# x queued first, rotary tables made later, 12 taps of a matrix tile on VectorE, statistics products inside z chunks

## The chip, the core and the metric

The kernel runs on one core of a Trainium2 chip. The metric is the device time of one execution, in microseconds (us). TensorE (PE in the profile) multiplies matrices; VectorE (DVE), ScalarE (ACT) and GpSimd (POOL) work on tiles of 128 partitions; SyncE (SP) issues all the loads and stores.

## The reference, cut

A convolution layer, then an attention layer. Only the first is touched, and the rotary tables of the second.

```python
def conformer_conv_branch(h, w_in, b_in, conv_w, conv_b, norm_g, norm_b, w_out, b_out):
    proj = h @ w_in + b_in                     # (512,1024) @ (1024, 3*2048)
    val, glu_gate, z = jnp.split(proj, 3, axis=-1)
    u = val * jax.nn.sigmoid(glu_gate)
    u = lax.conv_general_dilated(u, conv_w[:, None, :], ...) + conv_b   # depthwise, causal, 31 taps
    u = jax.nn.silu(layer_norm(u, norm_g, norm_b))                      # over the 2048 channels
    u = u * jax.nn.silu(z)
    return u @ w_out + b_out
def rope_tables(positions, dtype):
    freqs = ROPE_THETA ** (-jnp.arange(0, 64, 2, dtype=jnp.float32) / 64)
    ang = positions.astype(jnp.float32)[..., None] * freqs
    return jnp.cos(ang).astype(dtype), jnp.sin(ang).astype(dtype)
```

## The kernel before, in words

Channels lie on partitions and the 512 positions on the free axis, so the 2048 channels of the convolution are 16 tiles. Each fp32 product is made of three matmuls: the operands are split into a high part (ScalarE copies to fp32r, `w_hi`, `xt_hi`) and the rest (GpSimd subtracts, `w_lo`; VectorE, `xt_lo`). The weights come in chunks of 128 columns, 512 KB each: SyncE loads a chunk into one of two raw buffers once both splits of the chunk before last are done, ScalarE makes `w_hi` (line 710), GpSimd `w_lo` (line 566), and TensorE spends 24 matmuls of 512 columns on it (`columns`, matmuls at line 1416). The slots of `w_hi` and `w_lo` are four. All orders are written by hand, one program for each engine, with semaphores between them.

**Start.** SyncE queues x in four parts with the first two weight chunks between them, then the taps (`taps_raw`, 31 rows of 8 KB), six small vectors (`vec_raw`), `freq` and the positions (`pos_int`, broadcast to 128 partitions). All nine small transfers count on one semaphore, `small_landed`. TensorE turns x with 32 transposes, does chunk 0, then `small_transposes` (16 of the taps at line 1434, one of the vectors at 1437), which waits for all nine, then chunk 1. ScalarE evacuates the turned taps and vectors (`conv_w_hi`, `vec`), which the biases of the first evacuation need. VectorE makes the angles of the rotary tables in 13 chained operations (lines 1045 to 1059), then copies the taps (1062, 1063), then begins to convolve. ScalarE makes `sin` and `cos` from the angles.

**Value and gate.** For tile t, chunk 2t gives `val` and chunk 2t+1 `sig` (ScalarE), and GpSimd multiplies them to `u` (line 571).

**Convolution.** 12 of the 16 tiles are convolved on VectorE, one instruction a tap (line 1093), two tiles at a time taking turns, but the first 14 taps and the last dozen run as one chain. Tiles 3 and 9 are shared: ScalarE multiplies (744), GpSimd adds (593). Tiles 12 and 13 are convolved on TensorE after chunk 31: each tap is a diagonal matrix, three matmuls, 31 taps, in four groups (`convolve`); GpSimd makes `diag_hi` (606) and ScalarE `diag_lo` (753). VectorE adds up all tiles (`csum`, lines 1076 and 1078).

**z chunks and statistics.** TensorE does 16 chunks of z. Ahead of chunk 10 it sums `csum` over the channels (line 1488), ahead of chunk 13 the squares (1495), ahead of chunk 14 it spreads the reciprocal deviation (1481). In between VectorE centres the tiles (1146), ScalarE squares them (814), VectorE adds the even squares (1152) and GpSimd the odd ones (621), GpSimd takes the power (642) and ScalarE makes `rstd_diag` (853).

**Branch and output projection.** For each tile VectorE scales (1176), ScalarE does silu (820), VectorE multiplies with z (1183), ScalarE makes `g_hi` (826), VectorE `g_lo` (1187). The output projection takes two tiles of g for each chunk of weights; in the loop of 16 tiles ScalarE also splits output chunks 2 and 3, and the chunks from 4 on come after it.

## Time and profile before

| | |
|---|---|
| median of 3 runs | 876.32 us (876.02 to 878.18) |
| the profiled execution: time | 877.75 us |
| the profiled execution: span from first to last instruction | 876.0 us |
| mean granted TensorE clock | 0.995 |
| TensorE busy | 851.5 us, 97% of the span |
| VectorE, ScalarE, GpSimd busy | 601.8, 398.2, 471.8 us |

The span is what the profile's clock covers; 1.75 us of the execution lie around it. TensorE's busy share is near the whole, so what matters is which of its gaps go and which come, and how many matmuls it has to do.

### The profile page before, as it was taken

The numbers are of one execution on the slowest core, as the hardware profiler recorded it, in microseconds if no ns is written. First come the engines' busy times: TensorE is split into PE (matmuls) and PEld (weight loads), VectorE is DVE, ScalarE is ACT, GpSimd is POOL, SyncE is SP. The second block draws the span as 40 slices with busy tenths as digits, with TensorE's granted clock in tenths as the row PEclk, the third lists the DMA queues.
The fourth block names the chain that finished last, engine by engine and source line by source line (L and its number), as shares of the span: only waits on it lengthen the run. The fifth ranks groups of instructions, "written<-read, shape, count | busy, mean of one in ns | idle before, by whom it ended". The sixth has DMA issues, their size and how long they took to land.

```text
span 876.0 us, 11846 instructions
## 1 busy us (share of the span) xinstructions
PE 851.5 (97%) x4083; PEld 708.4 (81%) x4083; DVE 601.8 (69%) x1089; ACT 398.2 (45%) x690; POOL 471.8 (54%) x260
## 2 busy tenths in 40 slices
PE   6999999999999999999999999999999999989996
PEld 5788888888888788788898788788888898878885
DVE  2899999999999749321723380157977878787207
ACT  3555444444564467431332443255555546554110
POOL 3577988896996572493454456142432433136431
PEclk9899999999999999999999999999999999999999
DMA  6232333330024323453143324323123230224212
GB/s 214 75 96 74 97 96 96 96 97 25 1 73 125 109 80 103 142 186 98 49 121 109 97 72 133 84 73 84 42 56 84 72 84 15 70 97 145 97 48 97
DMA packets 111399, 78.99 MB, mean 90 GB/s; under 512 B 14071, under 2 KB 98141, under 8 KB 111325
## 3 DMA queue, kind: packets, MB, share of 16 engines
q1 hardware_dynamic: 111356, 78.44, 30.2%
q8 instruction: 24, 0.39, 0.2%
q14 instruction: 19, 0.16, 0.1%
HBM read 71.87 MB, written 2.10 MB: 84 GB/s over the span
## 4 chain that ended last, share of the span: by engine, by line
PE 95%; DMA 2%; DVE 1%; SPq 1%; issue 1%; ACT 1%; DVEq 0%; ACTq 0%
PE bank L1416 89%; PE bank L1679 2%; DMA pos_int<-in_positions_dram 2%; PE bank L1668 1%; PE bank L1669 1%; PE bank L1554 0%; SPq L419 0%; DVE fg_lo L1400 0%; SPq L412 0%; PE bank L1434 0%; PE bank L1606 0%; PE bank L1495 0%; DVE pt_lo L1355 0%; SPq L416 0%; ACT prob L970 0%
## 5 line engine op out<-in xcount | busy, mean ns | idle before, releaser
L566 POOL TENSOR_TENSOR w_lo<-w_raw,w_hi 128x1024 fp32r<-128x1024 f32 x103 | 253.6, 2472 | 189.3 <-ACT w_hi L710 163.4
L1093 DVE SCALAR_TENSOR_TENSOR bank<-u,conv_w,bank 128x512 f32<-128x512 f32 x348 | 233.8, 759 | 0.9
L710 ACT ACTIVATE w_hi<-w_raw 128x1024 fp32r<-128x1024 f32 x103 | 107.0, 1054 | 117.6 <-PE bank L1416 66.8
L1416 PE MATMUL bank<-xt_hi,w_lo 128*128 128x512 f32 x384 | 153.6, 400 | 1.4 <-DVE xt_lo L1032 1.4
L1416 PE MATMUL bank<-xt_lo,w_hi 128*128 128x512 f32 x384 | 152.4, 397 | 0.0
L1416 PE MATMUL bank<-xt_hi,w_hi 128*128 128x512 f32 x384 | 152.3, 397 | 0.0
L1416 PEld LDWEIGHTS bank<-xt_hi,w_lo 128*128 128x128 f32 x384 | 73.1, 190 | 19.3 <-DVE xt_lo L1032 1.8
L1416 PEld LDWEIGHTS bank<-xt_lo,w_hi 128*128 128x128 f32 x384 | 72.9, 190 | 17.2 <-issue 0.5
L1416 PEld LDWEIGHTS bank<-xt_hi,w_hi 128*128 128x128 f32 x384 | 72.9, 190 | 17.2
L593 POOL TENSOR_TENSOR acc<-acc,tap_product 128x512 f32<-128x512 f32 x60 | 77.9, 1299 | 8.5 <-ACT tap_product L744 1.6
L664 POOL TENSOR_TENSOR bundle_lo<-bundle_raw,bundle_hi 128x1024 fp32r<-128x1024 f32 (+1 forms) x16 | 47.0, 2957 | 63.1 <-ACT bundle_hi L905 63.1
L1416 PE MATMUL bank<-ht_hi,w_lo 128*128 128x512 f32 (+1 forms) x208 | 76.4, 367 | 0.0
L1416 PE MATMUL bank<-ht_lo,w_hi 128*128 128x512 f32 (+1 forms) x208 | 75.8, 365 | 0.0
L1416 PE MATMUL bank<-ht_hi,w_hi 128*128 128x512 f32 (+1 forms) x208 | 75.8, 365 | 0.0
L1209 DVE SCALAR_TENSOR_TENSOR bank<-res,bank 128x512 f32<-128x512 f32 x16 | 11.0, 690 | 93.7 <-PE bank L1416 63.3
L744 ACT ACTIVATE tap_product<-u,conv_w 128x512 f32<-128x512 f32 x60 | 41.8, 719 | 33.5 <-POOL acc L593 33.4
L970 ACT ACTIVATE prob<-prob,neg_top 128x512 f32<-128x512 f32 (+1 forms) x64 | 35.5, 556 | 42.3 <-DVE neg_top L1314 42.3
L1416 PE MATMUL bank<-w_hi,g_lo 128*128 128x512 f32 x128 | 51.1, 399 | 1.6 <-issue 1.6
L1416 PE MATMUL bank<-w_hi,fg_lo 128*128 128x512 f32 x128 | 50.9, 398 | 1.2 <-DVE fg_lo L1400 1.2
L1416 PE MATMUL bank<-w_hi,fg_hi 128*128 128x512 f32 x128 | 50.6, 395 | 0.0
L1416 PE MATMUL bank<-w_hi,g_hi 128*128 128x512 f32 x128 | 50.6, 395 | 0.0
L1416 PE MATMUL bank<-w_lo,fg_hi 128*128 128x512 f32 x128 | 50.3, 393 | 0.0
(196 smaller groups left out, 1795.1 us busy)
## 6 DMA issues: line engine op xcount, KB each, us to landing
w_raw<-in_a_w_in_dram SPq DMA_DIRECT2D x48, 512.0 KB, 3.7
w_raw<-in_b_w_in_dram SPq DMA_DIRECT2D x20, 512.0 KB, 3.6
w_raw<-in_a_w_out_dram SPq DMA_DIRECT2D x16, 512.0 KB, 4.1
w_raw<-in_b_w_out_dram SPq DMA_DIRECT2D x16, 512.0 KB, 3.5
bundle_raw<-in_b_w_uq_dram SPq DMA_DIRECT2D x16, 256.0 KB, 3.8
x_in<-in_x_dram SPq DMA_DIRECT2D x4, 512.0 KB, 5.8
res<-in_x_dram SPq DMA_DIRECT2D x4, 512.0 KB, 5.0
bundle_raw<-in_kv_w_uk_dram SPq DMA_DIRECT2D x8, 256.0 KB, 2.9
```

Of the source, the lines that this page charges most:

```text
L566: nc.gpsimd.tensor_tensor(w_lo[slot][:], w_raw[raw][:], w_hi[slot][:].bitcast(F32), ALU.subtract).then_inc(w_lo_ready, 1)
L593: nc.gpsimd.tensor_tensor(acc[:, t, :], acc[:, t, :], tap_product[n % 2][:], ALU.add).then_inc(product_added, 1)
L664: nc.gpsimd.tensor_tensor(bundle_lo[slot][part][:], bundle_raw[:, lo:hi], bundle_hi[slot][part][:].bitcast(F32), ALU.subtract).then_inc(bu ...
L710: nc.scalar.activation(w_hi[slot][:], w_raw[raw][:], ACT.Copy).then_inc(w_hi_ready, 1)
L744: nc.scalar.activation(tap_product[n % 2][:], u[:, t, k:k + SEQ], ACT.Copy, scale=tap).then_inc(product_ready, 1)
L970: nc.scalar.activation(block_, block_, ACT.Exp, bias=neg_top[:, b:b + 1], scale=SM_SCALE, accum_out=denom[:, b:b + 1]).then_inc(exp_done, 1)
L1093: nc.vector.scalar_tensor_tensor(out=bank[CONV_BANK[slot]][:] if k < TAPS - 1 else acc[:, t, :], in0=u[:, t, k:k + SEQ], scalar=conv_w[:, ...
L1209: nc.vector.scalar_tensor_tensor(out=total[:], in0=rows_half, scalar=scale, in1=total[:], op0=ALU.mult, op1=ALU.add).then_inc(y_step, 1)
L1416: last = nc.tensor.matmul(out_ap, a, b, start=(start and n == 0 and m == 0), stop=(stop and n == len(parts) - 1 and m == 2))
L1668: nc.tensor.matmul(bank[score_bank[i]][:, 0:n], stack[:, cut], kr_lo[:, 0:n], start=False, stop=False)
L1669: nc.tensor.matmul(bank[score_bank[i]][:, 0:n], stack[:, cut], kr_hi[:, 0:n], start=False, stop=True).then_inc(scores_done, 1)
L1679: last = nc.tensor.transpose(bank[to_bank][:, first + k * P:first + (k + 1) * P], prob[:, (prob_at[b] + k) * P:(prob_at[b] + k + 1) * P], ...
```

## The change

What it does, in the order of the program:

- SyncE queues the four parts of x first, then weight chunks 0 and 1. `freq` and `pos_int` leave the first group (now seven transfers on `small_landed`) and are loaded after the z chunks.
- ScalarE splits chunks 2 and 3 before it waits for the turned taps. `small_transposes` comes after chunk 1 instead of chunk 0.
- VectorE makes the angles after the branch loop instead of at the start; ScalarE makes `sin` and `cos` after output chunk 11.
- Tile 12: TensorE does 19 of the 31 taps (four groups of 5, 5, 5, 4), ScalarE puts the biased sum back into its bank, and VectorE adds the other 12 taps as a thirteenth entry of its list. Tile 13 keeps all 31 taps on TensorE; the diagonals of its last 12 are made during the value and gate chunks, in iteration 6.
- The four groups between the convolutions take 12 shared-tap products instead of 20; the rest go to z chunks 0 to 8 (before 0 to 4).
- The products of the statistics stand inside z chunks: the mean in chunk 11 after 6 of its 8 parts, the squares in chunk 14 after 5, the spread in chunk 15 after 2. The last odd square is added by VectorE instead of GpSimd.
- GpSimd takes the power before it splits output chunk 0; ScalarE splits output chunk 4 inside the branch loop (at tile 13).

```diff
-        TAP_GROUPS = tuple(range(8 * g, min(8 * g + 8, TAPS)) for g in range(4))
+        MATRIX_TAPS = (19, TAPS)
+        TAP_GROUPS = tuple(range(a, b) for a, b in zip((0, 5, 10, 15, 19), (5, 10, 15, 19, 31)))
+        SHARED_SLOTS = len(TAP_GROUPS) - 1
-        PAIR_SHARE, MATRIX_SHARE, Z_SHARE = 3, 20, 2
+        PAIR_SHARE, MATRIX_SHARE, Z_SHARE = 3, 12, 2
-        MEAN_AT, VAR_AT, SPREAD_AT = 10, 13, 14
-        SQUARES = {13: range(0, 8), 14: range(8, CT)}
+        MEAN_AT, VAR_AT, SPREAD_AT = (11, 5), (14, 4), (15, 1)
+        SQUARES = {14: range(0, 8), 15: range(8, CT)}
...
             for r in range(RT):
                 sp.dma_start(x_in[:, r, :], x_rows[:, r, :]).then_inc(x_landed[r], 16)
-                if r % 2 == 1:
-                    w = r // 2
-                    load_columns(w, w_in_a, w * CONV_WIDTH)
+            for w in range(2):
+                load_columns(w, w_in_a, w * CONV_WIDTH)
...
-            sp.dma_start(freq[:], rope_freq).then_inc(small_landed, 16)
-            sp.dma_start(pos_int[:], positions.broadcast_to([P, SEQ])).then_inc(small_landed, 16)
...
+            sp.wait_ge(diag_used, SHARED_SLOTS)
+            sp.dma_start(freq[:], rope_freq).then_inc(table_landed, 16)
+            sp.dma_start(pos_int[:], positions.broadcast_to([P, SEQ])).then_inc(table_landed, 16)
...
-                if q % 4 == 3:
-                    split_hi(q // 4, q // 4, q // 4, 16)
+                if q == 5:
+                    split_hi(0, 0, 0, 16)
+            split_hi(1, 1, 1, 16)
+            for w in range(2):
+                split_hi(2 + w, w, 2 + w, 32)
...
+                if t == 13:
+                    output_split(SLOTS)
...
-                coming = list(VECTOR_TILES)
+                coming = list(VECTOR_TILES) + [MATRIX_TILES[0]]
...
+                    product(bank[out_bank][:], parts[:n], True, False)
+                    between[1]()
+                    product(bank[out_bank][:], parts[n:], False, True).then_inc(w_used, 1)
...
-                        if isinstance(c, int) and c == 0:
+                        if isinstance(c, int) and c == 1:
                             small_transposes()
```

The end of VectorE's convolution, before: the last chain of tile 15, the sums of the matrix and shared tiles ahead of it (`bank<-bank,acc`).

```order
L1093 SCALAR_TENSOR_TENSOR acc<-u,conv_w,bank 128x512
L1093 SCALAR_TENSOR_TENSOR bank<-u,conv_w,bank 128x512 x2
L1078 TENSOR_TENSOR bank<-bank,acc 128x512 x5
L1093 SCALAR_TENSOR_TENSOR bank<-u,conv_w,bank 128x512 x11
L1093 SCALAR_TENSOR_TENSOR acc<-u,conv_w,bank 128x512
L1078 TENSOR_TENSOR csum<-bank,acc 128x512
```

The same place in the changed program.

```order
L1087 SCALAR_TENSOR_TENSOR acc<-u,conv_w,bank 128x512
L1087 SCALAR_TENSOR_TENSOR bank<-u,conv_w,bank 128x512 x2
L1071 TENSOR_TENSOR bank<-bank,acc 128x512
L1087 SCALAR_TENSOR_TENSOR bank<-u,conv_w,bank 128x512 x12
L1071 TENSOR_TENSOR bank<-bank,acc 128x512 x3
L1087 SCALAR_TENSOR_TENSOR bank<-u,conv_w,bank 128x512 x9
L1087 SCALAR_TENSOR_TENSOR acc<-u,conv_w,bank 128x512
L1087 SCALAR_TENSOR_TENSOR bank<-u,conv_w,bank 128x512
L1087 SCALAR_TENSOR_TENSOR acc<-u,conv_w,bank 128x512
L1071 TENSOR_TENSOR bank<-bank,acc 128x512
L1071 TENSOR_TENSOR csum<-bank,acc 128x512
```

After the third row, where 12 taps and one sum followed the five sums, 24 taps now stand, those of tile 12 between those of tile 15; the sums are six either way. On TensorE the mean now stands inside z chunk 11 (`w_hi_75`, `w_lo_79` are that chunk's slots, `w_hi_72` the next one's).

```order
L1439 MATMUL bank<-xt_hi,w_hi_75 128x512
L1517 MATMUL bank<-csum,ones 128x512
L1439 MATMUL bank<-xt_hi,w_lo_79 128x512
L1439 MATMUL bank<-xt_lo,w_hi_75 128x512
L1439 MATMUL bank<-xt_hi,w_hi_75 128x512
L1439 MATMUL bank<-xt_hi,w_lo_79 128x512
L1439 MATMUL bank<-xt_lo,w_hi_75 128x512
L1439 MATMUL bank<-xt_hi,w_hi_75 128x512
L1439 MATMUL bank<-xt_hi,w_lo_76 128x512
```

Before, six whole chunks (144 matmuls of 512 columns) stood behind the mean; now six matmuls of chunk 11 and four chunks, 102.

## Rows read from the trace of the kernel before

**Rows 1.** The page: busy time by engine; the chain that ended last.

```profile
PE 851.5 (97%) x4083; PEld 708.4 (81%) x4083; DVE 601.8 (69%) x1089; ACT 398.2 (45%) x690; POOL 471.8 (54%) x260
...
PE 95%; DMA 2%; DVE 1%; SPq 1%; issue 1%; ACT 1%; DVEq 0%; ACTq 0%
```

**Rows 2.** Timeline of PE at the start: start us, us, what [idle before <-releaser].

```profile
14.76 0.50 PE L1416 MATMUL bank<-xt_hi,w_lo 128*128 128x512 f32 x1 [1.41 <-DVE xt_lo L1032]
...
23.72 1.85 PE L1434 MATMUL bank<-ident,taps_raw 31*128 31x31 f32 x16 [3.11 <-DMA pos_int<-in_positions_dram]
...
33.58 0.40 PE L1416 MATMUL bank<-xt_hi,w_lo 128*128 128x512 f32 x1
```

**Rows 3.** Windows: stretch, PE PEld DVE ACT POOL busy (count), PEclk, DMA share, GB/s.

```profile
25.90:30.30 4.40, 4.40 (x12) 3.43 (x11) 4.27 (x4) 4.30 (x6) 2.79 (x2) 0.50 0.02 4
...
100.00:150.00 50.00, 50.00 (x217) 40.52 (x215) 50.00 (x77) 23.70 (x33) 43.87 (x28) 1.00 0.35 103
```

**Rows 4.** DMA view: weight chunk 1, issued at 3.76; GB/s in 40 slices of 12 to 28 us.

```profile
w_raw<-in_a_w_in_dram SPq DMA_DIRECT2D x1, 512.0 KB, 8.6
...
GB/s 122 113 84 187 262 329 334 147 33 41 20 20 41 20 20 41 20 20 136 251 275 339 284 47 19 26 22 22 8 22 22 22 22 22 9 41 0 0 0 0
```

**Rows 5.** Timeline at the start: first split of weights, Sigmoid's table, sig, u.

```profile
8.39 1.06 ACT L710 ACTIVATE w_hi<-w_raw 128x1024 fp32r<-128x1024 f32 x1
...
9.53 2.36 POOL L566 TENSOR_TENSOR w_lo<-w_raw,w_hi 128x1024 fp32r<-128x1024 f32 x1 [6.17 <-ACT w_hi L710]
...
28.97 1.28 ACT L719 ACT_TABLE_LOAD   x1
...
33.78 0.69 ACT L719 ACTIVATE sig<-bank,vec 128x512 f32<-128x512 f32 x1 [3.53 <-PE bank L1416]
...
34.55 1.57 POOL L571 TENSOR_TENSOR u<-val,sig 128x512 f32<-128x512 f32 x1 [2.03 <-ACT sig L719]
```

**Rows 6.** Timeline of DVE: first angle, first tap, taps in pairs, the end.

```profile
23.70 0.43 DVE L1045 CAST pos<-pos_int 128x512 f32<-128x512 int32 x1 [8.99 <-DMA pos_int<-in_positions_dram]
...
36.33 0.81 DVE L1088 TENSOR_SCALAR bank<-u,conv_w,vec 128x512 f32<-128x512 f32 x1 [0.20 <-POOL u L571]
...
48.07 21.16 DVE L1093 SCALAR_TENSOR_TENSOR bank<-u,conv_w,bank 128x512 f32<-128x512 f32 x32
...
285.53 8.66 DVE L1093 SCALAR_TENSOR_TENSOR bank<-u,conv_w,bank 128x512 f32<-128x512 f32 x11
...
295.01 0.69 DVE L1078 TENSOR_TENSOR csum<-bank,acc 128x512 f32<-128x512 f32 x1
```

**Rows 7.** PE: the 62 matmuls with diag_lo (ns; first and last start).

```profile
L1416 PE MATMUL bank<-cu_hi,diag_lo x62: 388/394/407, 200.9 to 243.5; 128*128 128x512 f32 x62
```

**Rows 8.** Timeline of PE: the mean, the spread, output chunk 4.

```profile
299.94 1.02 PE L1488 MATMUL bank<-csum,ones 128*128 128x512 f32 x2
...
324.88 1.02 PE L1481 MATMUL bank<-rstd_diag,ones 128*128 128x512 f32 x2
...
361.05 0.47 PE L1416 MATMUL bank<-w_hi,g_lo 128*128 128x512 f32 x1 [1.56 <-issue]
```

**Rows 9.** Timelines behind the mean: last square, diagonals; branch loop (ACT, DVE).

```profile
314.73 0.64 ACT L814 ACTIVATE sq<-acc 128x512 f32<-128x512 f32 x1 [0.56 <-DVE acc L1146]
...
322.78 1.28 ACT L853 ACTIVATE rstd_diag<-ident,rstd_cols 128x128 f32<-128x128 f32 x4 [3.36 <-POOL rstd_cols L642]
...
331.60 1.06 ACT L710 ACTIVATE w_hi<-w_raw 128x1024 fp32r<-128x1024 f32 x1 [1.54 <-PE bank L1416]
...
357.46 1.05 ACT L710 ACTIVATE w_hi<-w_raw 128x1024 fp32r<-128x1024 f32 x1
...
329.26 0.68 DVE L1187 TENSOR_TENSOR g_lo<-bank,g_hi 128x512 fp32r<-128x512 f32 x1
```

**Rows 10.** Waits of 300 to 421 us: waiting <- releaser, us in total, times, longest.

```profile
DVE bank L1209 <- POOL res L659: 30.4, 1, 30.4
```

**Rows 11.** The page's row of the shared products on POOL: busy us, mean ns.

```profile
L593 POOL TENSOR_TENSOR acc<-acc,tap_product 128x512 f32<-128x512 f32 x60 | 77.9, 1299 | 8.5 <-ACT tap_product L744 1.6
```

More of the change, by code:

```diff
@@ L600, in conv_matrices @@
                 n = hi - lo
-                if m == 0:
-                    pool.wait_ge(taps_hi_ready, 1)
-                else:
+                pool.wait_ge(taps_hi_ready, 1)
+                if m == 1 and g < SHARED_SLOTS:
                     pool.wait_ge(diag_used, g + 1)
@@ L814, in square @@
                     nc.scalar.activation(sq[t % 4][:], acc[:, t, :], ACT.Square
-                                         ).then_inc((squared_even, squared_odd)[t % 2], 1)
+                                         ).then_inc(squared_odd if t % 2 == 1 and t < CT - 1 else squared_even, 1)
             def branch_silu(t):
@@ L868, in _ @@
                     branch_hi(t - 1)
-            for k in range(SLOTS, CT):
+            for k in range(SLOTS + 1, CT):
                 output_split(k)
@@ L875, in _ @@
                                          ).then_inc(res_scaled, 1)
+                if k == 11:
+                    act.wait_ge(angles_ready, 1)
+                    nc.scalar.activation(sin[:], angle[:], ACT.Sin).then_inc(rope_ready, 1)
+                    nc.scalar.activation(cos[:], angle_c[:], ACT.Sin).then_inc(rope_ready, 1)
             act.wait_ge(g_lo_ready, CT)
@@ L1198, in _, with chained @@
                     branch_lo(t - 2)
+            steps = [0]
+            def chained(instruction):
+                instruction.then_inc(table_step, 1)
+                steps[0] += 1
+                dve.wait_ge(table_step, steps[0])
+            dve.wait_ge(table_landed, 32)
+            dve.wait_ge(rstd_spread, 1)
+            chained(nc.vector.tensor_copy(pos[:], pos_int[:]))
+            chained(nc.vector.tensor_scalar(angle[:], pos[:], freq[:, 0:1], None, ALU.mult))
+            chained(nc.vector.tensor_scalar(turns[:], angle[:], 1.0 / TWO_PI, ROUNDER, ALU.mult, ALU.add))
+            chained(nc.vector.tensor_scalar(turns[:], turns[:], -ROUNDER, None, ALU.add))
+            for part in (PI_A, PI_B, PI_C):
+                chained(nc.vector.scalar_tensor_tensor(out=angle[:], in0=turns[:], scalar=-part, in1=angle[:],
+                                                       op0=ALU.mult, op1=ALU.add))
+            chained(nc.vector.tensor_scalar(angle_c[:], angle[:], 0.5 * np.pi, None, ALU.add))
+            chained(nc.vector.tensor_scalar(turns[:], angle_c[:], PI_SAFE, -TWO_PI, ALU.is_gt, ALU.mult))
+            chained(nc.vector.tensor_tensor(angle_c[:], angle_c[:], turns[:], ALU.add))
+            chained(nc.vector.tensor_scalar(angle_c[:], angle_c[:], PI_SAFE, -PI_SAFE, ALU.min, ALU.max))
+            chained(nc.vector.tensor_scalar(angle[:], angle[:], PI_SAFE, -PI_SAFE, ALU.min, ALU.max))
+            nc.vector.tensor_scalar(angle[:], angle[:], freq[:, 1:2], None, ALU.mult).then_inc(angles_ready, 1)
             HALF_STEPS, ROW_STEPS = 2, 4
@@ L1438, in small_transposes, with columns @@
                                     ).then_inc(vec_turned, 1)
-            def columns(c, slot, out_bank, bank_free, hi, lo):
+            def columns(c, slot, out_bank, bank_free, hi, lo, between=None):
                 pe.wait_ge(w_hi_ready, c + 1)
@@ L1446, in columns @@
                           hi[:, k, :], lo[:, k, :]) for k in range(KD)]
-                product(bank[out_bank][:], parts, True, True).then_inc(w_used, 1)
+                if between:
+                    n = between[0] + 1
+                    product(bank[out_bank][:], parts[:n], True, False)
+                    between[1]()
+                    product(bank[out_bank][:], parts[n:], False, True).then_inc(w_used, 1)
+                else:
+                    product(bank[out_bank][:], parts, True, True).then_inc(w_used, 1)
             def value_gate(j):
```

158 lines of the change are left out of this document (73 added, 85 removed).

## Prediction

> **What bounds the kernel now.** I read the page first. TensorE is busy 97% of the span and the chain that ended last is 95% TensorE [rows 1], so only two things shorten the kernel: fewer matmuls, or fewer and shorter gaps between them. Then the timeline of TensorE at the start [rows 2]: after chunk 0 it stands still for 3.11 us, until the last small transfer is there at 23.7, does the small transposes, and then runs chunk 1 at a granted clock of 0.50, the 1.2 GHz level [rows 3]; chunk 2 begins at 33.58. From there to the output projection nothing interrupts it: a stretch of 50 us is 50.00 us busy [rows 3]. The matmuls with diagonals give its pace, 62 with `diag_lo` starting from 200.9 to 243.5, three matmuls apart: 42.6 / 183 = 0.2328 us a matmul [rows 7]. So a chunk of 24 is 5.59 us. The last view is VectorE's: it convolves without a break from 36.33 and has `csum` at 295.01 + 0.69 = 295.70, while TensorE asks for it at 299.94 [rows 6, 8]. VectorE thus has 4.2 us to spare. That is the number on which this change turns.
>
> **Matmuls removed.** 12 taps of tile 12, three matmuls each: 36 x 0.2328 = 8.4 us. Nothing else leaves TensorE.
>
> **The start.** Everything ahead of the taps is the same 3 MB in another order, and it had landed at 3.76 + 8.6 = 12.4 [rows 4]. With x first, chunk 0 comes fifth: I put it at 10.9 (between 9.9 and 11.5; before, its split began at 8.39). From its landing to the first matmul are ScalarE's 1.06, GpSimd's 2.36 and 0.1 of handing over [rows 5], so TensorE begins at 14.4 (13.4 to 15.1), against 14.76. Chunks 0 and 1 then run in one piece to 14.4 + 11.2 + 0.2 = 25.8. The small transposes come next. They took 1.9 us at half clock [rows 2]; at full clock between 1 and 1.9, I take 1.5. Chunk 2 begins at about 27.4, if its weights are there.
>
> Are they? The GB/s row has, after the bursts, a tail at 20 to 22 GB/s that lasts until the small transfers land, with a second one behind it [rows 4]: one long transfer at a low rate, 248 KB / 22 = 11.3 us, which is `taps_raw` begun when the first six were through (12.4 + 11.3 = 23.7). The release at 23.7 bears the name of `pos_int` [rows 2] because it was queued last. The weights of chunks 2 and 3 are behind that tail too. Without `pos_int` and `freq` the small ones land about 0.8 us sooner, 22.9; chunk 2 at about 23.8, split by 23.8 + 3.5 = 27.3. Both meet at 27.4 to 27.5; if the tail doesn't shrink, 28.2. Gain of TensorE at chunk 2: 33.6 - 27.5 = 6.1 us.
>
> The Trainium skill, DMA: Bandwidth & Descriptors, section on why a DMA increments its semaphore by 16, says that a copy is spread over the largest number of engines up to 16 that divides its slowest dimension, so that 31 rows go to one engine. By that rule the tail is the taps and stays; by the label of the row it would be the positions and go. By either, the wait is gone, because TensorE asks only at 25.8: the sum would differ by 0.1 us.
>
> **VectorE's start.** The angles are off its front, but it must wait for u of tile 0. From the end of the transposes (27.2, between 26.8 and 27.8): two small evacuations and `val`, together 1.5 us (each under 0.7, the size of `sig`), Sigmoid's table 1.28, `sig` 0.77, GpSimd's product 1.57, handing over 0.2 [rows 5, 6]: 5.3 us. First tap at 32.5, against 36.33: 3.8 us sooner. With pairs at 21.16 / 32 = 0.66 us a tap it never again waits for u.
>
> **VectorE's end.** In the place of 11 chained taps (285.53 to 294.23, 0.79 each) and their last one stand 24, of which 22 in pairs: 22 x 0.66 + 2 x 0.79 = 16.1 us against 12 x 0.79 = 9.5, so 6.6; I take 6.4, since of the six sums, as many as before, fewer stand in one chain. `csum` is ready at 295.7 - 3.8 + 6.4 = 298.3.
>
> **Where they meet.** TensorE would ask for the mean at 299.94 - 6.1 (start) - 8.4 (taps) + 42 x 0.2328 = 9.8 (it stands 42 matmuls further on) = 295.2; I allow half a microsecond more, since in iteration 6 GpSimd makes 12 diagonals ahead of its splits: 1536 columns, at most 1.5 x 2.36 = 3.5 us [rows 5], of which its free share (6.1 us in 50, 1.4 in an iteration of 11.2 [rows 3]) and its lead of a chunk cover most. So 295.7, and VectorE is 2.6 us late. TensorE waits there, the new gap. Any small loss before (the 0.5, chunk 2 at 28.2) only shortens this wait.
>
> **Behind the mean.** TensorE has 42 matmuls fewer to do, so the end moves by 298.3 - 299.9 - 9.8 = -11.4 us, if the chain behind keeps up. Its distances, from the mean (M): the last square ends at M + 15.4 [rows 8, 9], VectorE adds it by M + 16.2 and TensorE asks at M + 0.9 + 69 x 0.2328 = M + 16.9. From there the eight products take 1.7, then come ScalarE's four diagonals, 1.28 [rows 9], and ahead of them steps of four columns on VectorE and GpSimd, for which and for handing over I take 1.5: M + 21.4; TensorE asks at M + 22.1. The first `g_lo` ends 5.1 us after the spread begins (329.26 + 0.68 - 324.88); TensorE asks 0.9 + 18 x 0.2328 = 5.0 after it. All three fit, with 0.7, 0.7 and 0 to spare, and the third may cost 0.1.
>
> Before, output chunk 4 was split only behind the branch loop, at 357.46, and TensorE stood 1.56 us for it [rows 8, 9]. Now it is split at tile 13, about 24.4 us after the spread, ready 3.5 later at 27.9, wanted at 5.1 + 22.35 = 27.4: 0.5 us. Chunk 5 comes behind the loop, 357.46 - 324.88 - 1.4 (ScalarE's wait for TensorE at 331.60 is gone) = 31.2, ready at 34.7, wanted at 33.5: 1.2 us. The stall moves one chunk and is about as long, 1.7 against 1.6. Net with the 0.1: +0.2.
>
> **Moved at no cost.** Angles, 11.3 us of chained work (23.70 to about 35): VectorE waits 30.4 us behind the branch loop [rows 10]. `sin` and `cos` with a table, about 2.5 us on ScalarE in the output projection, where a chunk takes TensorE 5.6 and ScalarE 1.06. Without those covers they would cost 11 and 2.5 us. The DMAs of positions stand ahead of output chunk 0, which is split only at M + 15.
>
> **Sum.** -11.4 + 0.2 = -11.2. Against the profiled execution's 877.75: 866.5. The median of the runs lies 1.4 below that execution, so 865.1.
>
> **Rivals.**
> 1. *TensorE stays the bound* at the mean, since VectorE starts or ends sooner than I count: then -8.4 - 6.1 + 0.5 + 0.2 = -13.8, 862.5. For it: only 2.6 us decide. Against: the taps' 0.66 is steady over 32. 15%.
> 2. *The clock falls in a new gap.* Before, a stand of 3.1 us was followed by the 1.2 GHz level; the 12 matmuls of 25.9 to 30.3 took 4.4 us instead of 2.8 and the transposes were slow as well [rows 2, 3]. Now there are two stands of 2.6 to 2.9 us: between the last transpose of x and chunk 0, and at the mean. Yet the first matmul after the stand of 1.56 us took 0.47, near the 0.39 of the others [rows 7, 8]. Each fall costs some 2 us: 867.1, with both 869. 25%. The Trainium skill, TensorE: Matmul & The Clock Gate, the part on oscillation, says that gaps while waiting return the array to the lower clock; by that rule this is the case to fear, and this trace agrees with it in one gap of two.
> 3. *The chain behind the mean misses.* It had 1.2 us and more and has 0.7 and 0. If the squares and the spread are each late by 1 us: 867. 12%.
> 4. *Slower.* GpSimd becomes the bound of the z chunks: 9 of them now carry two shared additions, 2.47 + 2 x 1.3 = 5.1 of TensorE's 5.6 us [rows 11]. If an addition took 1.57, as a product did at the start [rows 5], they would be even. To lose all the 13.8 us of the first rival over 9 chunks each must take 7.1 us, 2.3 an addition. Then 877 and more. 2%. That the edits do nothing measurable: 2%.
>
> My own case has 44%, with 863.5 to 866.5. A difference of 0.3% (2.6 us) is what a measurement tells from none. Range over the cases: 861.5 to 869.5. Faster 0.95, within 0.02, slower 0.03.
>
> **What will show it.** Right: chunk 2 at 27 to 28; no wait at the small transposes; 150 matmuls with diagonals; first tap at 32 to 33; a gap of 2 to 3 us on TensorE ahead of the mean at 298, released by VectorE; a stall of 1 to 1.5 at output chunk 5 and a smaller one at chunk 4; clock 1.00 past the start. Wrong: slow matmuls from 14 to 20 or behind the mean; a gap of over 0.3 us at the squares or the spread; VectorE idle ahead of the mean product.

## The result, and the profile after

| | before | after | forecast |
|---|---|---|---|
| median, same chip, 12 runs each | 878.13 us (874.36 to 879.53) | 872.22 us (871.07 to 875.58) | 865.1 us |
| ratio | | 0.9938, 95% interval 0.9926 to 0.9951 | 0.987 |
| profiled execution: time, span | 877.75, 876.0 us | 871.58, 869.6 us | 866.5, 864.8 us |
| chunk 2 begins | 33.58 | 28.32 | 27.5 |
| VectorE's first tap | 36.33 | 33.31 | 32.5 |
| mean product begins | 299.94 | 298.94 | 298.3 |
| spread begins | 324.88 | 321.17 | 320.4 |
| output projection begins | 336.9 | 326.48 | 325.5 |

The change is a gain, but about half of the forecast one: 6.2 us between the profiled executions (5.9 between the medians), against 11.2. The measured 872.22 us lie above the forecast range, which ended at 869.5. The table is the quickest way to see where the rest is. Up to the output projection the kernel is 1.0 us behind its forecast. From there to the end it took 876.0 - 336.9 = 539.1 us before and takes 869.6 - 326.48 = 543.1 after. The forecast had 539.3. So 3.8 of the 4.8 us of span that are missing lie behind the first matmul of the output projection, where I had looked only at the weights of chunks 4 and 5.

In what follows a stand is a time in which TensorE has nothing to run because it waits, and slow matmuls are those of 512 columns that start 0.42 to 0.43 us apart instead of 0.23.

The list of TensorE's waits after, whole (engine, line, releaser: sum, times, longest):

```profile
PE bank L1450 <- DMA x_in<-in_x_dram: 4.1, 1, 4.1
PE bank L1439 <- POOL w_lo L578: 4.0, 1, 4.0
PE bank L1439 <- ACT z_a L809: 3.8, 1, 3.8
PE bank L1517 <- DVE csum L1071: 2.0, 1, 2.0
PE bank L1439 <- DVE q_lo L1368: 1.8, 2, 1.5
PE bank L1439 <- DVE pt_lo L1378: 1.5, 1, 1.5
PE bank L1439 <- DVE v_lo L1362: 0.6, 1, 0.6
PE bank L1439 <- issue: 0.4, 1, 0.4
```

The second and the fourth row are the two stands that I had expected, 4.0 ahead of chunk 0 and 2.0 ahead of the mean. The third is not in the forecast at all: `z_a`, the gate z as ScalarE writes it out of its bank. The last, 0.4 us at 95.91, is the half microsecond that the prediction allowed for iteration 6: GpSimd ends the low part of that chunk at 95.8. The chain that ended last has changed from TensorE alone [rows 1] to TensorE and VectorE:

```profile
PE 62%; DVE 31%; issue 2%; DMA 2%; POOL 1%; ACT 1%; SPq 0%; DVEq 0%; POOLq 0%
```

VectorE's 31% are its convolution, from the first tap to `csum`. Each microsecond at its start or in its taps now reaches the end of the kernel.

The timeline of TensorE at the start and at the small transposes (start, duration, name, in brackets the idle time before), for comparison with [rows 2]:

```profile
4.14 6.12 PE L1450 MATMUL bank<-ident,x_in 128*128 128x128 f32 x32 [4.14 <-DMA x_in<-in_x_dram]
14.27 0.47 PE L1439 MATMUL bank<-xt_hi,w_lo 128*128 128x512 f32 x1 [4.01 <-POOL w_lo L578]
14.58 0.39 PE L1439 MATMUL bank<-xt_lo,w_hi 128*128 128x512 f32 x1
14.81 0.42 PE L1439 MATMUL bank<-xt_hi,w_hi 128*128 128x512 f32 x1
15.04 0.62 PE L1439 MATMUL bank<-xt_hi,w_lo 128*128 128x512 f32 x1
15.46 0.63 PE L1439 MATMUL bank<-xt_lo,w_hi 128*128 128x512 f32 x1
...
18.44 0.40 PE L1439 MATMUL bank<-xt_hi,w_hi 128*128 128x512 f32 x1
...
27.13 1.18 PE L1457 MATMUL bank<-ident,taps_raw 31*128 31x31 f32 x16
28.24 0.31 PE L1460 MATMUL bank<-ident,vec_raw 102*128 102x102 f32 x1
28.32 0.48 PE L1439 MATMUL bank<-xt_hi,w_lo 128*128 128x512 f32 x1
```

Chunk 0 begins where it was expected (14.4 forecast). From 15.04 to 18.44 the starts are 0.42 to 0.43 us apart instead of 0.23: eight matmuls at the 1.2 GHz level, 3.4 us instead of 1.9, so 1.5 us lost. No wait stands ahead of the small transposes or of chunk 2 any more; both were ready.

VectorE's last stretch, the row after the first tap first:

```profile
33.31 0.81 DVE L1079 TENSOR_SCALAR bank<-u,conv_w,vec 128x512 f32<-128x512 f32 x1 [3.10 <-POOL u L583]
...
279.31 7.98 DVE L1087 SCALAR_TENSOR_TENSOR bank<-u,conv_w,bank 128x512 f32<-128x512 f32 x12
287.21 2.15 DVE L1071 TENSOR_TENSOR bank<-bank,acc 128x512 f32<-128x512 f32 x3
289.27 6.01 DVE L1087 SCALAR_TENSOR_TENSOR bank<-u,conv_w,bank 128x512 f32<-128x512 f32 x9
...
298.10 0.69 DVE L1071 TENSOR_TENSOR csum<-bank,acc 128x512 f32<-128x512 f32 x1
```

Twelve taps in 7.98 us are 0.665 each: the taps of two tiles taking turns run at the pace of a pair, as the sum had it. And TensorE from the mean to the output projection:

```profile
298.94 1.10 PE L1517 MATMUL bank<-csum,ones 128*128 128x512 f32 x2 [1.98 <-DVE csum L1071]
...
321.17 1.02 PE L1512 MATMUL bank<-rstd_diag,ones 128*128 128x512 f32 x2
...
325.97 0.40 PE L1439 MATMUL bank<-xt_hi,w_hi 128*128 128x512 f32 x1
326.48 0.47 PE L1439 MATMUL bank<-w_hi,g_lo 128*128 128x512 f32 x1
...
328.48 0.40 PE L1439 MATMUL bank<-w_hi,g_hi 128*128 128x512 f32 x1
332.73 0.79 PE L1439 MATMUL bank<-w_hi,g_lo 128*128 128x512 f32 x1 [3.85 <-ACT z_a L809]
333.32 0.63 PE L1439 MATMUL bank<-w_lo,g_hi 128*128 128x512 f32 x1
333.74 0.63 PE L1439 MATMUL bank<-w_hi,g_hi 128*128 128x512 f32 x1
334.17 0.63 PE L1439 MATMUL bank<-w_hi,g_lo 128*128 128x512 f32 x1
...
335.88 0.42 PE L1439 MATMUL bank<-w_lo,g_hi 128*128 128x512 f32 x1
336.13 0.40 PE L1439 MATMUL bank<-w_hi,g_hi 128*128 128x512 f32 x1
```

No wait at the squares or the spread, and hardly one ahead of the first `g_lo`. But the tenth matmul of the output projection stands 3.85 us, and those behind it are slow again: from 332.73 to 336.13 eight starts take 3.4 us instead of 1.9. The granted clock shows both places (columns: the stretch; busy time and count of PE, PEld, DVE, ACT and POOL; PEclk, DMA share, GB/s). It is 0.66 and 0.75 over stretches that hold matmuls at both levels:

```profile
15.00:20.00 5.00, 5.00 (x16) 3.93 (x15) 0.00 (x0) 0.00 (x0) 1.45 (x1) 0.66 0.49 144
330.00:335.00 5.00, 2.27 (x5) 1.82 (x6) 4.90 (x9) 3.61 (x7) 0.00 (x0) 0.75 0.63 209
```

What is the tenth matmul? The output projection writes four blocks of 128 rows, one bank each, with three matmuls a block for each tile of g: the tenth is the first one into bank 3. That bank holds z chunk 15, until ScalarE has evacuated it. ScalarE's timeline says when it does:

```profile
331.51 0.59 ACT L836 ACTIVATE g_hi<-bank 128x512 fp32r<-128x512 f32 x1
331.98 0.69 ACT L809 ACTIVATE z_a<-bank,vec 128x512 f32<-128x512 f32 x1
332.75 0.75 ACT L830 ACTIVATE bank<-bank,vec 128x512 f32<-128x512 f32 x1
```

The evacuation stands at tile 6 of the branch loop, in both kernels. Chunk 15 had been complete on TensorE at 326.4. In the trace of before the same evacuation and the tenth matmul are these:

```profile
337.14 0.69 ACT L799 ACTIVATE z_a<-bank,vec 128x512 f32<-128x512 f32 x1
339.03 0.40 PE L1416 MATMUL bank<-w_hi,g_lo 128*128 128x512 f32 x1
```

There the evacuation ended at 337.14 + 0.69 = 337.8, and TensorE asked for the bank at 339.0: 1.2 us to spare. Counted from the spread, ScalarE is ready 12.9 us behind it before and 332.67 - 321.17 = 11.5 behind it after; TensorE asks 14.1 behind it before and 328.9 - 321.17 = 7.7 after. Moving the statistics later into the z chunks moved everything that hangs on them, this evacuation too, towards the output projection.

### The profile page after: what moved, and what is told of

It is laid out like the page before. It is cut to its first block, busy times and chain, and to the rows that moved or that the text cites. A ratio compares the mean times of both kernels' runs of the same rounds, so it can differ in the third digit from the quotient of the medians.

```text
span 869.6 us, 11782 instructions
## 1 busy us (share of the span) xinstructions
PE 843.8 (97%) x4047; PEld 701.0 (81%) x4047; DVE 619.4 (71%) x1102; ACT 390.9 (45%) x676; POOL 468.5 (54%) x260
## 4 chain that ended last, share of the span: by engine, by line
PE 62%; DVE 31%; issue 2%; DMA 2%; POOL 1%; ACT 1%; SPq 0%; DVEq 0%; POOLq 0%
PE bank L1439 57%; DVE bank L1087 27%; DMA w_raw<-in_a_w_in_dram 2%; PE bank L1708 2%; PE bank L1698 1%; PE bank L1697 1%; DVE bank L1079 1%; DVE bank L1071 1%; POOL w_lo L578 1%; PE bank L1583 0%; DVE pt_lo L1378 0%; DVE bank L1173 0%; ACT w_hi L722 0%; DVE bank L1180 0%; DVE g_lo L1184 0%
## 5 line engine op out<-in xcount | busy, mean ns | idle before, releaser
L1087 DVE SCALAR_TENSOR_TENSOR bank<-u,conv_w,bank 128x512 f32<-128x512 f32 x359 | 239.8, 745 | 0.5
L1439 PEld LDWEIGHTS bank<-xt_hi,w_lo 128*128 128x128 f32 x384 | 72.7, 189 | 22.2 <-DVE xt_lo L1050 4.2
L1439 PE MATMUL bank<-w_lo,g_hi 128*128 128x512 f32 x128 | 50.8, 397 | 0.0
```

What stands on the lines that cost most here:

```text
L1087: nc.vector.scalar_tensor_tensor(out=inner[:] if k < TAPS - 1 else acc[:, t, :], in0=u[:, t, k:k + SEQ], scalar=conv_w[:, column:column + ...
L1439: last = nc.tensor.matmul(out_ap, a, b, start=(start and n == 0 and m == 0), stop=(stop and n == len(parts) - 1 and m == 2))
```

## The experiments

Kernels ran on one chip in these groups, each with the kernel before beside them: keep_z15_early, vector_15_taps, fill_before_chunk0 and stats_at_old_places; chunks_4_5_early, early_and_filled, early_filled_9_taps and one_tap; keep_z15_again, small_after_chunk_0, x_queued_as_before and chunks_4_5_again; old_queue_4_5_early and chunks_4_5_third. Ratios are to the kernel before on the same chip. In keep_z15_early and all that build on it the line numbers behind the edit are one less than in the changed kernel.

**keep_z15_early.** One line moved: ScalarE evacuates z chunk 15 at tile 3 of the branch loop instead of tile 6.

```diff
                 if t == 3:
                     output_split(2)
                     keep_z(CT - 2)
-                if t == 6:
                     keep_z(CT - 1)
```

Expected: 

> The changed kernel with one line moved: ScalarE evacuates z chunk 15 (the bank that the output projection's fourth row block needs) at tile 3 of the branch loop instead of tile 6. Theory: the 3.85 us wait of TensorE at 328.9 and the nine slow matmuls behind it (about 1.5 us) are what the prediction lacked; both go, and about 1.3 us come back as a wait for the weights of output chunk 5. Span 869.6 - 5.3 + 1.3 = 865.6, ratio to the kernel before about 0.989. Rival: the wait only stood in for another (chunks 4 and 5, g_lo), and nearly all of it comes back elsewhere: span 868.5 or more, ratio 0.993.

Measured: 867.57 us, ratio 0.9883 (0.9866 to 0.9899), span 866.7. The wait for `z_a` is gone and the tenth matmul of the output projection starts 0.24 us after the ninth. In its place stand the two waits that I had forecast for output chunks 4 and 5:

```profile
350.75 0.47 PE L1438 MATMUL bank<-w_hi,g_lo 128*128 128x512 f32 x1 [0.23 <-issue]
357.63 0.47 PE L1438 MATMUL bank<-w_hi,g_lo 128*128 128x512 f32 x1 [1.03 <-issue]
```

In the changed kernel the longer stand before them had hidden these. The theory held: one line, moved by three tiles, takes the ratio from 0.9938 to 0.9883, nearly as much again as the whole change did (each ratio is to the kernel before on its own chip). The 1.1 us by which the span is longer than expected are at another place, the mean:

```profile
298.67 2.04 PE L1516 MATMUL bank<-csum,ones 128*128 128x512 f32 x2 [1.98 <-DVE csum L1070]
299.73 1.42 PE L1438 MATMUL bank<-xt_hi,w_lo 128*128 128x512 f32 x1
300.94 0.63 PE L1438 MATMUL bank<-xt_lo,w_hi 128*128 128x512 f32 x1
301.37 0.63 PE L1438 MATMUL bank<-xt_hi,w_hi 128*128 128x512 f32 x1
```

The same stand of 1.98 us as in the changed kernel, but here with slow matmuls behind it; the spread comes 23.8 instead of 22.2 us after the mean, 1.6 us more. Run once more (below), this kernel had no slow matmuls at the mean and took 866.0 - 299.58 = 566.4 us behind it, against a forecast of 864.8 - 298.3 = 566.5 and the 869.6 - 298.94 = 570.7 of the changed kernel.

**stats_at_old_places.** The changed kernel with the products of the statistics nearly where they were, behind the first of the eight parts of z chunks 10, 13 and 14.

```diff
-        MEAN_AT, VAR_AT, SPREAD_AT = (11, 5), (14, 4), (15, 1)
-        SQUARES = {14: range(0, 8), 15: range(8, CT)}
+        MEAN_AT, VAR_AT, SPREAD_AT = (10, 0), (13, 0), (14, 0)
+        SQUARES = {13: range(0, 8), 14: range(8, CT)}
```

Expected: 

> The changed kernel with the three statistics products back at (nearly) their old places: after the first part of z chunks 10, 13 and 14. Theory: the mean stays where VectorE lets it be (298.9), but 39 matmuls more stand behind it (+9.1 us), and the output projection begins long enough after the spread that the wait for z chunk 15 and its slow matmuls go (-5.35): span 873.3, with a wait of some 11 us at the mean. Rival: the places matter little because TensorE does the same work in any order: span 869 to 870.

Measured: 876.81 us, ratio 0.9990 (0.9981 to 1.0000), span 873.0. The profiled execution, 874.96 us, is the shortest of the ten, so that its span meets the expected 873.3 is in part luck; the median of the ten spans is 875.0. TensorE stands at the mean for as long as it is now early:

```profile
298.34 2.05 PE L1517 MATMUL bank<-csum,ones 128*128 128x512 f32 x2 [10.63 <-DVE csum L1071]
```

The start and the taps bring nothing without a later place for the mean. And there is no wait for `z_a`: the output projection begins 11.4 us after the spread here and 5.3 in the changed kernel. So it is the move of the statistics that made the evacuation late.

**one_tap.** The changed kernel with one tap of tile 12 on VectorE instead of 12.

```diff
-        MATRIX_TAPS = (19, TAPS)
-        TAP_GROUPS = tuple(range(a, b) for a, b in zip((0, 5, 10, 15, 19), (5, 10, 15, 19, 31)))
+        MATRIX_TAPS = (30, TAPS)
+        TAP_GROUPS = tuple(range(a, b) for a, b in zip((0, 8, 16, 24, 30), (8, 16, 24, 30, 31)))
```

Expected: 

> The changed kernel with the 12 taps taken back but for one: tile 12 has 30 of 31 taps on TensorE, one on VectorE; start, statistics and branch loop stay as changed. TensorE gets 33 matmuls, 33 x 0.2328 = 7.7 us; VectorE loses 11 taps, about 7 us. By my account of the change TensorE waits 2.0 us for csum with 12 taps and not at all with one, so the mean comes 7.7 - 2.0 = 5.7 us later, and everything behind, the stand of 3.85 us in the output projection too, stays as it is: span 869.6 + 5.7 = 875.3 us, ratio to the kernel before 0.998 to 0.999. So all parts of the change but the taps would be worth only 1 us as it stands. The rival, that the stand in the output projection comes from what the taps brought (VectorE late, and with it ScalarE), gives no stand there and 875.3 - 5.4 = 869.9 us.

Measured: 877.54 us, ratio 1.0008 (0.9999 to 1.0017), span 876.0. The mean begins at 304.64, without a wait, which is the expected place (298.9 - 2.0 + 7.7 = 304.6). In part that is luck: chunk 2 came 0.7 us later than in the changed kernel, and the wait of 0.4 us at iteration 6 was gone. The stand for `z_a` is the same to a hundredth:

```profile
338.35 0.80 PE L1439 MATMUL bank<-w_hi,g_lo 128*128 128x512 f32 x1 [3.85 <-ACT z_a L809]
```

So neither the taps nor VectorE's lateness make it. Without the taps, then, what the start wins and what this stand costs cancel. The 0.7 us over the expectation are the clock: 13 slow matmuls behind the stand, seven in the changed kernel, 1.2 us more; and none behind a stand of 1.54 us in the attention part, where the changed kernel had some, 0.5 us less.

**vector_15_taps.** 15 taps of tile 12 on VectorE.

```diff
-        MATRIX_TAPS = (19, TAPS)
-        TAP_GROUPS = tuple(range(a, b) for a, b in zip((0, 5, 10, 15, 19), (5, 10, 15, 19, 31)))
+        MATRIX_TAPS = (16, TAPS)
+        TAP_GROUPS = tuple(range(a, b) for a, b in zip((0, 4, 8, 12, 16), (4, 8, 12, 16, 31)))
```

Expected: 

> The changed kernel with 15 instead of 12 taps of tile 12 on VectorE (16 on TensorE, groups of 4). TensorE has 9 matmuls (2.1 us) less, VectorE three taps (2.0 us) more. Theory: since VectorE is the bound ahead of the mean, the mean moves 2.0 us later, TensorE waits 2.0 + 4.1 = 6 us there, and the span grows by 2 (871.6) or more if the clock falls. Rival: TensorE's work sets the end: the span shrinks by 2.1 (867.5).

Measured: 877.85 us, ratio 1.0003 (0.9990 to 1.0016), span 876.2. VectorE is the bound at the mean (wait of 4.13 us, mean 1.6 us later), so the direction is that of my theory and against the rival. The size is not: 6.6 us longer, where 2.0 were expected. 1.6 of them are the later mean; 1.6 are slow matmuls behind the longer stand there; 3.3 come behind the start of the output projection (13 slow matmuls behind the wait for `z_a`, 1.2 us more than seven; 2.0 us at two places where TensorE waits for `qr_stack`, a transfer in the attention part that the changed kernel doesn't wait for). Why that transfer was late stays open. The wait at the mean is 4.13 us and not 6 because TensorE asks only 0.5 us sooner than in the changed kernel, not 2.1: with 15 diagonals to make in iteration 6, GpSimd lets TensorE stand 1.27 us there instead of 0.41, and 0.77 us more at a diagonal of a matrix tile (217.36). The experiment says that more taps lose, not what one tap costs.

**fill_before_chunk0.** 30 transposes of `x_in` into a free bank, thrown away, in the stand ahead of chunk 0.

```diff
+            for _ in range(30):
+                nc.tensor.transpose(bank[7][:, 0:P], x_in[:, RT - 1, 0:P], ident[:])
```

Expected: 

> The changed kernel with 30 needless transposes of x into a free bank between the last transpose of x and chunk 0 (3.3 us of the 4.0 us gap). Theory: the gap is what brings TensorE to the 1.2 GHz level from 15.0 to 18.4; filled, chunk 0 runs at full pace throughout, chunk 1 ends 1.7 us sooner, the first tap of VectorE and with it the mean come 1.6 us sooner: span 868.0. Rival: the fall has nothing to do with the gap, or merely moves to the stretch around the small transposes: span 869.6, and 873 if the transposes run past the arrival of the weights.

Measured: 869.90 us, ratio 0.9915 (0.9898 to 0.9933), span 868.0, as expected. No matmul of chunk 0 is slow, the small transposes begin at 25.66 instead of 27.13, the first tap at 31.8 instead of 33.3, and the mean comes 1.5 us sooner. So the fall of the clock behind the stand ahead of chunk 0 costs 1.5 us up to the mean, and 1.6 in the span. Chunk 2 began at 27.52, and the last 0.45 us before it were a wait for its weights: they were there when the forecast had them, at 27.4 to 27.5.

**chunks_4_5_early.** keep_z15_early, and ScalarE splits output chunk 4 at tile 12 and chunk 5 at tile 15 of the branch loop.

```diff
-                if t == 13:
-                    output_split(SLOTS)
+                if t in (12, 15):
+                    output_split(SLOTS + t // 15)
...
-            for k in range(SLOTS + 1, CT):
+            for k in range(SLOTS + 2, CT):
```

Expected: 

> This kernel is keep_z15_early with one more step: ScalarE splits output chunk 4 at tile 12 and chunk 5 at tile 15 of the branch loop, instead of chunk 4 at tile 13 and chunk 5 behind the loop. Two theories of what is left in the output projection. (a) The two stands that keep_z15_early showed, 0.23 us at chunk 4 and 1.03 us at chunk 5, are late splits only: then both go and nothing else moves, the span is 866.7 - 1.3 = 865.4 us, ratio to the kernel before 0.987. (b) ScalarE has no free room left in the branch loop, so that each split of 1.06 us that is put ahead of its silu and g_hi work makes the operands g of the output projection late instead: the span stays within 0.4 us of 866.7 or grows, with new stands of about 1 us at the last tiles of g.

Measured: 866.14 us, ratio 0.9887 (0.9868 to 0.9906), span 864.3. Both waits are gone, but the ratio is no lower than that of keep_z15_early on another chip, so both were run once more side by side. Expected of the two: 

> keep_z15_early once more, as the base for the three kernels beside it on the same chip. Time 0.988 of the kernel before, span 865.4 us if the clock holds after the stand of 2.0 us at the mean, 866.7 us if it falls there as it did in the first profile of this kernel; which of the two is open, since the same stand left the clock up in two other kernels.

> chunks_4_5_early once more beside keep_z15_again. If the two stands of 0.23 and 1.03 us in the output projection are worth their length, 1.3 us less than keep_z15_again, a ratio lower by 0.0014; if ScalarE's order in the branch loop takes it back, level with it.

Measured: keep_z15_again 868.28 us, ratio 0.9890 (0.9875 to 0.9904), span 866.0; chunks_4_5_again 865.42 us, ratio 0.9861 (0.9846 to 0.9875), span 863.0. Side by side the runs of the two, four each, do not overlap (867.29 to 868.47 and 864.80 to 865.62). Behind the mean the two take 566.4 and 564.6 us, 1.8 less where 1.3 were expected; the remaining 1.2 us lie ahead of the mean, where one had 12 slow matmuls at chunk 0 and the other eight. The early splits pay.

**early_and_filled.** chunks_4_5_early with the 30 transposes.

Expected: 

> chunks_4_5_early with the 30 dummy transposes ahead of chunk 0 of fill_before_chunk0. If the start and the output projection are independent (my theory), the start gives the same 1.6 us as it gave there: VectorE's first tap at 31.8 instead of 33.3, csum 1.5 us sooner, span 865.4 - 1.6 = 863.8 us, ratio 0.985. If in addition the shorter stand at the mean (1.3 us instead of 2.0) keeps the clock up there, where in keep_z15_early it fell and cost 1.3 us, 862.5 us. The rival, that the time saved at the start is waited for again at the mean because something other than VectorE is late there, gives 865.4 us and a stand of over 2.5 us at the mean.

Measured: 864.28 us, ratio 0.9859 (0.9844 to 0.9874), span 862.0, mean clock 0.999. The mean comes 1.7 us sooner than in chunks_4_5_early, at 297.36, with a wait of 0.90 us, and no matmul of chunk 0 or behind the mean is slow. The start and the output projection are independent. That the span fell by 2.3 rather than 1.7 is the clock at one more place: both kernels have a stand of 1.54 us in the attention part (`pt_lo`), at 763.38 and 761.82. In chunks_4_5_early the granted clock behind it was 0.53 for 3.5 us, here 1.00, and from there to the end the two take 100.9 and 100.1 us.

**early_filled_9_taps.** The same with 9 taps of tile 12 on VectorE (`MATRIX_TAPS = (22, TAPS)`, groups of 6, 6, 5, 5, 9).

Expected: 

> early_and_filled with 9 taps of tile 12 on VectorE instead of 12 (22 on TensorE). TensorE gets 9 matmuls more, 9 x 0.2328 = 2.1 us, VectorE 3 taps less, 3 x 0.66 = 2.0 us. In early_and_filled VectorE should be about 1.3 us late at the mean; here TensorE asks 2.1 us later and VectorE is 2.0 sooner, so the stand is gone and the mean comes 2.1 - 1.3 = 0.8 us later: 864.6 us against 863.8 if no clock fell in the other, 864.6 against 863.8 or even level if one did. The rival, that 12 taps are past the balance (VectorE so late that every tap given back is a gain), gives a time below early_and_filled by 1 us or more.

Measured: 866.37 us, ratio 0.9878 (0.9861 to 0.9896), span 864.7. That the span is as expected (864.6) is half chance, since the kernel beside it was shorter than expected: the mean begins at 299.87 instead of 297.36, 2.5 us later where 1.2 were due (2.1 - 0.9). The rest is the clock, at a place where it held in the others: behind a stand of 1.26 us at chunk 2 nine matmuls were slow, some 1.6 us. `csum` is ready at 296.14 and TensorE asks 3.7 us later, 2 us later even without these. So with nine taps TensorE is the bound again, as I expected, and the rival (twelve are too many) is out.

**small_after_chunk_0.** keep_z15_early with the small transposes behind chunk 0, as before.

```diff
-                        if isinstance(c, int) and c == 1:
+                        if isinstance(c, int) and c == 0:
                             small_transposes()
```

Expected: 

> keep_z15_early with one part of the start undone: the small transposes come after chunk 0 again, as in the kernel before; x is still queued first, and the positions and angles are still late. My theory: TensorE ends chunk 0 at about 21.6 us and the taps land at about 23, so it stands there for 1.3 us or more, and chunk 2 and VectorE's first tap come 1.3 to 1.5 us later than in keep_z15_again; because VectorE is the bound at the mean, all of it reaches the end: span 1.4 us longer, ratio 0.990, and up to 3 us longer if the clock falls in that stand. The rival, that this step was free (the stand at the mean of 2.0 us takes it up), gives no difference.

Measured: 869.56 us (867.00 to 872.74), ratio 0.9912 (0.9896 to 0.9928), against 0.9890 (0.9875 to 0.9904) beside it; the span of the profiled run is 865.2, 0.8 shorter. The two disagree, and the runs of this kernel are wide apart, so no verdict on the time. The trace still says something. TensorE does stand at the small transposes, 1.12 us:

```profile
23.51 1.17 PE L1456 MATMUL bank<-ident,taps_raw 31*128 31x31 f32 x16 [1.12 <-DMA vec_raw<-in_kv_norm_g_dram]
```

That wait ends at 23.5, where in the kernel before it ended at 23.7 [rows 2], although the positions are no longer in the group. So the tail ahead of the small transfers hardly shrank (the prediction had it end at 22.9): it is not the positions that made it. In the changed kernel that costs nothing, since TensorE asks at 27.

The trace corrects me on VectorE too: its first tap comes at 32.77, 1.2 us sooner than in keep_z15_again (33.94), not later. Tile 0's value and gate need the turned biases; with the transposes behind chunk 1, `val` of chunk 0 waits for them too (it starts at 29.72, here at 27.02) and stands in the chain to `u`. The move helps TensorE (chunk 2 at 28.94 instead of 30.36) and delays VectorE by 1.2 us. Where VectorE is the bound at the mean, as in the changed kernel, that delay counts; here `csum` was ready at 298.28 and TensorE asked last, at 298.77.

**x_queued_as_before.** keep_z15_early with the weight chunks between the parts of x again.

```diff
                 sp.dma_start(x_in[:, r, :], x_rows[:, r, :]).then_inc(x_landed[r], 16)
-            for w in range(2):
-                load_columns(w, w_in_a, w * CONV_WIDTH)
+                if r % 2 == 1:
+                    load_columns(r // 2, w_in_a, (r // 2) * CONV_WIDTH)
...
-                if q == 5:
+                if q == 3:
                     split_hi(0, 0, 0, 16)
```

Expected: 

> keep_z15_early with the other part of the start undone: the first two weight chunks are queued between the parts of x again, and ScalarE splits weight chunk 0 after the fourth piece of x. The small transposes stay after chunk 1. My theory: x is complete later and w_lo of chunk 0 sooner, and TensorE begins chunk 0 at about 14.8 us as in the kernel before, with a stand shorter than 4 us but broken up, so 0.5 us later than with x first; if the clock then falls as it does now the span is 0.5 us longer, and if it doesn't fall 1.2 us shorter. The rival, that x first is what gives the start its gain, gives 3 us or more.

Measured: 866.77 us (865.33 to 870.18), ratio 0.9888 (0.9875 to 0.9902), level with 0.9890 beside it; the profiled execution, span 863.5, is the shortest of the five. Both expectations were wrong. TensorE at its start:

```profile
9.00 2.33 PE L1449 MATMUL bank<-ident,x_in 128*128 128x128 f32 x16 [1.01 <-DMA x_in<-in_x_dram]
12.90 0.50 PE L1438 MATMUL bank<-xt_hi,w_lo 128*128 128x512 f32 x1 [1.57 <-DVE xt_lo L1049]
13.24 0.40 PE L1438 MATMUL bank<-xt_lo,w_hi 128*128 128x512 f32 x1
```

Chunk 0 begins 1.2 us sooner than with x first, and runs at full speed: the one long stand has become two short ones, since w_lo of chunk 0 is being made while the rest of x arrives. Whether that is a gain in time was still open, so:

**old_queue_4_5_early** and **chunks_4_5_third.** chunks_4_5_early with the same edit, and chunks_4_5_early again beside it.

Expected: 

> chunks_4_5_early with x_queued_as_before: the first two weight chunks stand between the parts of x again. In the profile x_queued_as_before began chunk 0 at 12.90 us with no slow matmuls behind it, against 14.07 and about 10 slow ones in keep_z15_again, and its span was 2.5 us shorter; timed, it was level. If x queued first costs time (the theory that the profile speaks for), this kernel takes 2 to 2.5 us less than chunks_4_5_third, ratio lower by 0.0025, about 0.9835. If it is level, as the timing says, the profile caught an early arrival of x and a repeated start is within 0.5 us.

> chunks_4_5_early as the base for the kernel beside it on the same chip: 0.986 to 0.989 of the kernel before, chunk 0 begins at 13.7 to 14.3 us behind a stand of 4 us, with 7 to 11 slow matmuls.

Measured: old_queue_4_5_early 865.64 us (862.76 to 866.15), ratio 0.9854 (0.9835 to 0.9874), span 861.0; chunks_4_5_third 866.81 us (865.39 to 868.59), ratio 0.9873 (0.9851 to 0.9895), span 863.9. Chunk 0 began at 12.54, again with no slow matmul. The profiled executions differ by 2.9 us and the medians by 1.2, with overlapping intervals; the profiled execution of old_queue_4_5_early is again the shortest of its five. That x first gains nothing is shown twice; that it costs something is likely and not settled. This kernel, early_and_filled and chunks_4_5_again have the lowest ratios, 0.9854, 0.9859 and 0.9861, and are not told apart.

## Why the prediction was wrong, step by step

**The step that failed** stands under "Behind the mean": "All three fit, with 0.7, 0.7 and 0 to spare". Three demands were checked, the squares, the spread and the first `g_lo`. There was a fourth, the bank that the output projection writes into. Its last holder, z chunk 15, is freed by ScalarE inside the branch loop, 1.2 us ahead of need in the kernel before. Cutting the distance from the spread to the output projection from 12.1 to 5.3 us made it late by 3.85 us, and the slow matmuls behind the stand added 1.5: 5.4 in all. In exchange the stands of 0.5 and 1.2 us that I had priced at chunks 4 and 5 didn't show, and the 1.56 us of before [rows 8] went. That is 5.4 - 1.6 = +3.8, where +4.0 was measured behind the first matmul of the output projection and the forecast had +0.2. Another +0.5 is the clock behind the stand of 1.54 us in the attention part: 0.59 granted from 768.8 to 772.2, and 1.00 at the same place of the kernel before. Small differences of -0.3 make up the rest. keep_z15_early shows this to be the cause; stats_at_old_places and one_tap show which part of the change brought it.

**The rivals and the range.** Rival 3, "The chain behind the mean misses", is the nearest to what happened. But it named the squares and the spread, which were in time, and its 867 comes from 1 us each. With the missing bank unpriced, the range ended at 869.5, and the time lies above it.

**The start.** Forecast -6.1 at chunk 2, measured 33.58 - 28.32 = -5.3. The weights and the small transfers were there, as argued. What failed is that chunks 0 and 1 would run at full clock: rival 2 came true at the first of its two places, for 1.5 us (its "some 2 us"), partly made good by transposes that took 1.2 instead of 1.5. The first tap followed, at 33.31 instead of 32.5. fill_before_chunk0 shows the price, 1.5 us at the mean. "With x first" was no cause of the gain: with the old queue the start is at least as good. I had added x first and the move of the small loads into one term and never asked what each was worth. Nor did the forecast see that small transposes behind chunk 1 put VectorE's first tap 1.2 us later than behind chunk 0 (small_after_chunk_0).

**VectorE's taps.** First tap to `csum` ready: 295.70 - 36.33 = 259.4 before, 298.79 - 33.31 = 265.5 after, +6.1, forecast 6.4. Right. So `csum` was 0.5 late on its forecast: 0.8 from the start, less 0.3 in the taps.

**The meeting.** Forecast 298.3 with a wait of 2.6, measured 298.94 with 1.98. VectorE is the bound there, as forecast; rival 1 fell. vector_15_taps and early_filled_9_taps show both sides of the balance, in the traces; their times also hold falls of the clock, 2.8 and 1.6 us. Rival 2's second place, the clock at the mean, was spared in the changed kernel and hit in one run of keep_z15_early, 1.6 us.

**Behind the mean**, to the first matmul of the output projection: 27.5 us, forecast 27.2. Squares and spread without a gap, the first `g_lo` 0.3 late (325.97 + 0.23 to 326.48), forecast 0.1.

**Chunks 4 and 5**: forecast 0.5 and 1.2, found once the bank was free, 0.23 and 1.03. **Moved at no cost**: right; no wait for the angles, `sin` or `cos` is in the list of TensorE's waits. **Rival 4**, GpSimd as the bound of the z chunks: not seen, no wait of TensorE there. GpSimd was late once past the start, in iteration 6, by 0.41 us, which the forecast had as 0.5.

The ledger of the span, forecast 864.8 to measured 869.6: mean +0.6, from there to the output projection +0.3, behind that 543.1 against 539.3, +3.8. The rest is rounding.

**From the execution to the median.** The prediction took 1.4 us off for the median, 865.1, from three runs of the kernel before. Over 12 runs the medians are 0.4 us above the profiled execution before and 0.6 after, so 2.0 of the 7.1 us between 865.1 and 872.22 are this step, and 5.1 the kernel.

## What to carry to other kernels

When a step is moved closer to its consumer, list everything that lies between the two on every engine and ask of each what it frees, banks and buffers as well as data; the distance in the old trace that is shorter than the cut is the new stand. The place to look is the last instruction that reads each bank that the next stage writes: here one row, 337.8 against 339.0, carried 3.8 of the 4.8 us of the miss. A term that is made of two edits should be priced edit by edit: undone one at a time, one of the two turned out to bring nothing.

## What the runs showed of the hardware

A stand can cost more than its length, and how much is not the same twice. Behind the stand for `z_a` (3.84 to 3.85 us in four kernels) seven to 13 matmuls of 512 columns started 0.42 to 0.43 us apart, every time. Behind the stand ahead of chunk 0 (3.24 to 4.04 us in ten profiles) it was seven to 14, every time; the granted clock was 0.51 from 15.0 to 18.4 us of the changed kernel, the 1.2 GHz level. The Trainium skill, "TensorE: Matmul & The Clock Gate", Part 1, gives 426.7 ns from start to start for 512 columns at the lower clock; the trace agrees, 0.42 to 0.43 us. Below 2 us it went either way. The 1.98 us at the mean left the pace as it was in the changed kernel and slowed the starts behind it in the first profile of keep_z15_early, for 1.6 us; in the second profile of that kernel it was 1.59 us and nothing slow followed. A stand of 1.26 us at chunk 2 had nine slow matmuls behind it in early_filled_9_taps; one of 1.38 us at the same place, in x_queued_as_before, had none. The clearest case is one that no change touched: a stand of 1.54 us in the attention part, ahead of the first product with `pt_hi` that waits for `pt_lo`, is in all 16 profiles. Behind it the pace fell in five of them, and from there to the end these took 100.5 to 100.9 us, the other eleven 100.1 to 100.4. At chunk 0 there were seven slow matmuls in the first profile of keep_z15_early and 12 in the second. Kernels that differ by a microsecond are told apart only side by side and over several runs.

Throwaway transposes held the clock at its upper level: with 30 of them, 3.44 us of the stand ahead of chunk 0, the granted clock was 1.00 up to 20 us, and the span 1.6 us shorter.
